# Expert products in tiles of 32 rows on PE's four column groups, in plain fp32, instead of tiles of 128 rows as three rounded products

## The chip, the cores and the metric

The kernel runs on one core of a Trainium2 chip. The metric is the device time of one execution in microseconds. The core has five engines, each with its own instruction stream: TensorE (PE, matrix products; PEld is its loading of the stationary operand), VectorE (DVE), ScalarE (ACT), GpSimdE (POOL) and SyncE (SP, which here only issues DMAs). They meet through semaphores. PE writes to PSUM, eight banks of 512 fp32 columns in each of 128 partitions.

## The reference

One inference step of a hybrid backbone: 128 context tokens and 512 latent tokens, 1024 channels, one layer. The token mixer (mLSTM, Fourier and pooling branches, merge gates, output projection) is not touched. The change is in the mixture of experts behind it:

```python
p_group = softmax(xf @ w_r1 + b_r1);  g_val, g_idx = top_k(p_group, 1)         # one of 4 groups
fine_sel = (einsum("nd,dge->nge", xf, w_r2) + b_r2)[g_idx]                      # its 4 experts
e_val, e_idx = top_k(fine_sel, 2);  e_w = softmax(e_val) * g_val
dense_w = one-hot of (g_idx * 4 + e_idx), weighted by e_w                       # (n, 16)
hid = einsum("nd,edf->nef", xt, w_up);  a, b = split(hid, 2)                    # 1024 -> 2 x 512
hid = silu(a) * b * dense_w
y = einsum("nef,efd->nd", hid, w_down)                                          # 512 -> 1024
```

Each of the 640 tokens goes to two of 16 experts, so there are 1280 rows of expert work. An expert has 4 MiB of up weights and 2 MiB of down weights in fp32, 96 MiB for all (100.7 MB). With the inputs of the reference the 16 experts get 91, 96, 151, 60, 67, 63, 51, 65, 45, 168, 132, 35, 66, 61, 55 and 74 rows. In tiles of 128 rows, one at least for each expert, that makes 19 tiles; in tiles of 32 rows it makes 3, 3, 5, 2, 3, 2, 2, 3, 2, 6, 5, 2, 3, 2, 2 and 3, together 48.

## The kernel before, in words

The program is straight code up to the output projection. Then, for each block of 128 tokens, LN1 and the router's logits are made, and the modulated rows u2 are written to a scratch tensor in HBM (`u2_rows`). DVE turns the logits into a slot for every (token, choice) (lines 1375 to 1462): experts get whole tiles in turn, so a slot is 128 times the tile number plus a place. It also writes `plan`, a row of integers with the expert of each tile and the number of tiles. PE makes from one-hot matrices the list of the tokens in each tile (`tile_idx`, line 1842).

The expert stage is a loop over tiles on each of PE, ACT, DVE and POOL (`expert_tile`, `gather`), with the trip count read from `plan`. SP has its own loop over experts.

For one tile: POOL gathers its 128 rows of u2 from HBM into `xg` (line 707). PE transposes them, eight 128x128 blocks, into PSUM (line 1851). ACT copies the transposed rows rounded to the fp32r format into `xgT_hi` (line 966), and DVE takes the remainder, the exact rows minus the rounded ones, into `xgT_lo` (line 1468). PE then multiplies with the weights, which stand in the same two parts. `split_product` adds hi*hi, hi*lo and lo*hi: 24 matmuls of 128x512 for the first half of the up weights, 24 for the second, and 24 for down (line 1859, and 1899 for the last tile). ACT makes the sigmoid of the first half (line 993), DVE multiplies by it and by the second half (lines 1484, 1491), PE transposes the hidden rows (line 1886), ACT rounds them (line 1008), DVE takes their remainder (line 1504). The down product of a tile is done one tile later, after the up product of the next, so that PE has work while the hidden rows are prepared. ACT copies its two banks to SBUF and stores 128 rows of 4 KiB in `y_slots` with one DMA (lines 980 to 984).

The weights of the next expert come by DMA, in pieces of 512 KiB, into three staging sets (SP, lines 596 and 609). When the next tile has another expert, ACT rounds each of 12 pieces into its hi place (lines 948, 953) and DVE makes its lo part (lines 1361, 1367). Both are in a conditional block, for which ACT and DVE read three entries of `plan` into registers for each tile (lines 987 to 991, 1476 to 1480). There are six places of 16 KiB per partition for hi and lo parts. A staging piece is free for the next load when its lo part is made.

At the end two rows of y per token are gathered from `y_slots`, weighted, added, and LN2 is made.

The column groups of PE are used in the kernel before too, in the product of the conditioning vectors with w_mod at line 1570. Its stationary operand has 32 columns, and four matmuls in turn write partitions 0 to 31, 32 to 63, 64 to 95 and 96 to 127 of one bank, 512 columns each, in plain fp32. In the profile a plain fp32 matmul has two records, an fp32r matmul one.

## Time and profile before

| | us |
|---|---|
| median of 3 runs (1094.95 to 1096.83) | 1095.31 |
| profiled execution | 1101.74 |
| its span, first to last instruction | 1099.9 |
| PE busy | 947.7 |
| DVE busy | 618.3 |
| ACT busy | 444.0 |
| mean granted PE clock | 0.926 |

The span is that of one profiled execution, 1.8 us shorter than its own device time. The time of the profiled execution is 6.4 us above the median of the runs. Busy times of matmuls overlap in the records, because the shown end of a matmul includes its way through the array. The distance from one start to the next tells what a matmul costs in a row of them. The chain that ended last goes back from the last instruction, at each step to what released it. A PEclk of 1.00 stands for 2.4 GHz and of 0.50 for 1.2 GHz. GB/s counts all DMA traffic of the core.

### The profile page before, as it was taken

Reading aid. Unit: us, or ns where it says so; the run is one execution under the profiler, and the core shown is the slowest. Engines: PE = TensorE matmul, PEld = TensorE weight load, DVE = VectorE, ACT = ScalarE, POOL = GpSimd, SP = SyncE. Lnnn points to the kernel's source line nnn. Section 1 sums busy time; section 2 is a strip of 40 time slices with the busy share of each in tenths; the row PEclk is TensorE's granted clock in tenths of the full one; section 3 lists DMA queues with packets and bytes.
Section 4 is the critical chain, followed back from the end, with each engine's and each line's share of the span. In section 5 each row is a group of like instructions: output and inputs, shape, how many; then the busy total and the mean of one; then the engine's idle time right before and its main releaser. Section 6 shows DMA issues by size and latency. Waiting matters only on the chain.

```text
span 1099.9 us, 13186 instructions
## 1 busy us (share of the span) xinstructions
PE 947.7 (86%) x4547; PEld 750.7 (68%) x4547; DVE 618.3 (56%) x886; ACT 444.0 (40%) x612; POOL 188.2 (17%) x148
## 2 busy tenths in 40 slices
PE   2799699999999999899989973699999999999800
PEld 0588588757777777676657753588888888888600
DVE  4616902023535447413168568486799964889458
ACT  1513212132433434312050003466788854787422
POOL 2386300000000000000005551111111110100056
PEclk9899897999999999989999985799999999999955
DMA  9967646220203013612062044694999977899552
GB/s 328 387 192 289 229 154 249 102 89 1 77 1 115 3 75 24 223 41 77 1 227 79 39 167 139 229 391 173 383 399 398 400 273 273 295 398 375 191 210 96
DMA packets 83107, 214.23 MB, mean 195 GB/s; under 512 B 7871, under 2 KB 9157, under 8 KB 79997
## 3 DMA queue, kind: packets, MB, share of 16 engines
q1 hardware_dynamic: 65072, 165.03, 41.5%
q10 hardware_dynamic: 11564, 26.90, 6.9%
q0 software_dynamic: 6432, 21.79, 5.4%
q8 instruction: 25, 0.41, 0.2%
q14 instruction: 14, 0.11, 0.0%
HBM read 190.59 MB, written 23.11 MB: 194 GB/s over the span
## 4 chain that ended last, share of the span: by engine, by line
PE 72%; DVE 12%; ACT 5%; DMA 4%; POOL 3%; issue 2%; SPq 1%; ACTq 0%; POOLq 0%; DVEq 0%
PE ps L1859 28%; PE ps L1633 23%; PE ps L1550 7%; PE ps L1619 3%; DMA ring<-in_w_mod 2%; PE ps L1750 2%; PE ps L1851 2%; PE ps L1687 1%; DVE R_x L1184 1%; ACT w_hi L772 1%; POOL R_x L666 1%; POOL R_x L665 1%; DMA out<-small 1%; PE ps L1570 1%; PE ps L1744 1%
## 5 line engine op out<-in xcount | busy, mean ns | idle before, releaser
L1633 PE MATMUL ps<-w_hi,uT_hi 128*128 128x512 f32 x320 | 133.4, 417 | 6.4 <-ACT R_x L869 2.5
L1139 DVE TENSOR_TENSOR w_lo<-ring,w_hi 128x1024 fp32r<-128x1024 f32 x52 | 67.0, 1317 | 126.1 <-ACT w_hi L772 124.8
L1633 PE MATMUL ps<-w_lo,uT_hi 128*128 128x512 f32 x320 | 126.8, 396 | 0.0
L687 POOL TENSOR_TENSOR R_u<-R_m 128x1024 f32<-128x1024 f32 x1 | 2.4, 2407 | 464.9 <-DVE R_m L1328 464.9
L1633 PEld LDWEIGHTS ps<-w_hi,uT_hi 128*128 128x128 f32 x320 | 61.0, 191 | 23.2 <-issue 4.0
L1361 DVE TENSOR_TENSOR wa_lo<-ring,wa_hi 128x1024 fp32r<-128x1024 f32 x64 | 74.1, 1219 | 4.4 <-ACT wa_hi L948 4.0
L1633 PEld LDWEIGHTS ps<-w_lo,uT_hi 128*128 128x128 f32 x320 | 60.9, 190 | 13.5
L1859 PE MATMUL ps<-wa_hi,xgT_hi 128*128 128x512 f32 x152 | 63.0, 415 | 5.2 <-DVE xgT_lo L1468 5.2
L869 ACT ACTIVATE R_x<-ps 128x512 f32<-128x512 f32 x30 | 17.9, 596 | 117.8 <-PE ps L1633 117.8
L772 ACT CAST w_hi<-ring 128x1024 fp32r<-128x1024 f32 x52 | 53.4, 1053 | 29.8 <-PE ps L1633 15.6
L1228 DVE TENSOR_TENSOR R_x<-R_x,ps 128x512 f32<-128x512 f32 x20 | 13.8, 688 | 91.0 <-PE ps L1550 90.7
L1633 PE MATMUL ps<-w_hi,uT_lo_a 128*128 128x512 f32 x160 | 64.5, 403 | 0.0
L1633 PE MATMUL ps<-w_hi,uT_lo_b 128*128 128x512 f32 x160 | 62.3, 390 | 0.0
L948 ACT CAST wa_hi<-ring 128x1024 fp32r<-128x1024 f32 x64 | 62.2, 1049 | 0.0
L703 POOL COPY idx_now<-tile_idx 128x1 int32 (+1 forms) x19 | 12.1, 634 | 287.1 <-PE ps L1851 264.3
L1859 PE MATMUL ps<-wa_hi,xgT_lo 128*128 128x512 f32 x152 | 61.1, 402 | 0.0
L1859 PE MATMUL ps<-wa_lo,xgT_hi 128*128 128x512 f32 x152 | 60.7, 399 | 0.0
L1859 PE MATMUL ps<-wb_hi,xgT_lo 128*128 128x512 f32 x152 | 59.3, 390 | 0.0
L1859 PE MATMUL ps<-wb_hi,xgT_hi 128*128 128x512 f32 x152 | 59.1, 389 | 0.0
L1859 PE MATMUL ps<-wb_lo,xgT_hi 128*128 128x512 f32 x152 | 59.1, 389 | 0.0
L1859 PE MATMUL ps<-wd_hi,hidT_hi 128*128 128x512 f32 x144 | 57.5, 399 | 0.0
L1859 PE MATMUL ps<-wd_hi,hidT_lo 128*128 128x512 f32 x144 | 56.2, 390 | 0.0
(356 smaller groups left out, 2216.7 us busy)
## 6 DMA issues: line engine op xcount, KB each, us to landing
ring<-in_w_up SPq DMA_DIRECT2D x64, 512.0 KB, 8.8
ring<-in_w_in SPq DMA_DIRECT2D x11, 2048.0 KB, 8.1
R_d<-in_w_up SPq DMA_DIRECT2D x32, 512.0 KB, 11.0
R_p<-in_w_down SPq DMA_DIRECT2D x32, 512.0 KB, 9.7
R_h<-in_w_down SPq DMA_DIRECT2D x32, 512.0 KB, 10.3
R_d<-in_w_mod SPq DMA_DIRECT2D x13, 1024.0 KB, 5.3
y_slots<-R_m ACTq DMA_DIRECT2D x19, 512.0 KB, 6.2
ring<-in_w_mod SPq DMA_DIRECT2D x8, 1024.0 KB, 21.0
```

Source lines behind the costliest of these rows:

```text
L772: nc.scalar.copy(split_weights(name)[0][:, 2 * q:2 * q + 2], weights(name)[:, 2 * q:2 * q + 2]).then_inc(S["w_hi_done"], 1)
L869: release(nc.scalar.activation(gate_sb[:, s % 2], bank(0), ACT.Sigmoid), ("G", s))
L948: nc.scalar.copy(w_hi_lo[i][0][:, q * PIECE:(q + 1) * PIECE], stage(i, q)).then_inc(S["up_hi"], 1)
L1139: tt(lo[:, at], weights(name)[:, at], hi[:, at].bitcast(F32), ALU.subtract).then_inc(S["w_split"], 1)
L1228: release(tt(dst if b == 1 else gated, gate_sb[:, s % 2], bank(1), ALU.mult), ("Y", s))
L1361: tt(w_hi_lo[i][1][:, at], stage(i, q), w_hi_lo[i][0][:, at].bitcast(F32), ALU.subtract).then_inc(S["up_split"], 1)
L1550: i = mm(out, lhs(k), rhs(k), start=(k == 0), stop=(k == n - 1))
L1619: i = mm(bank(gbank((part, c_, s)))[:, 0:HALF], (hi, lo)[a][:, k, c_ * P:(c_ + 1) * P], uT_parts(k)[b][:, half_cols(s)], start=(k == 0 and ...
L1633: i = mm(out, parts(k)[a][:, tok(j)], w[b][:, k], start=(k == 0 and a + b == 0), stop=(k == KD - 1 and b == 1))
L1750: i = mm(ps[:, b0 + h // 2, (h % 2) * HE:(h % 2) * HE + HE], lhs(h), rhs(h), start=True, stop=True)
L1851: i = tr(bank(4 + d // 4)[:, (d % 4) * P:(d % 4) * P + P], xg[:, d * P:(d + 1) * P], ident)
L1859: i = mm(out, lhs[a][:, k * P:(k + 1) * P], rhs[b][:, k, n0:n0 + BW], start=(k == 0 and a + b == 0), stop=(k == n - 1 and a == 1))
```

## The change

The expert stage is rewritten; the stages before it and after it compute the same.

- A tile has 32 rows (`SUB`), and two tiles make a pair, over which the loops run. A pair has 64 slots, and `MAXP` is the largest number of pairs. The slots, `plan` and `tile_idx` are made for this size.
- One gather fetches both tiles of a pair: each of its 128 indices names half a row of u2 (512 channels), twice the token plus the half. PE needs four transposes for them, ACT one copy of 128x512 (`copy_rows`).
- Nothing is rounded or split. For each 128 channels of the contraction, PE takes 32 rows as the stationary operand and streams 256 columns of weights through each of its four column groups, in plain fp32: 8 steps of four matmuls for up, 4 steps of four for down. The column groups hold different output channels, so that the hidden values are 128x128 and the output rows 128x256.
- The weights are loaded by SP into `staged`, two places of a whole expert used in turn, and copied from there to a third place, `expert_w`, from which PE reads. Of the 12 pieces of an expert ACT copies 0, 2, 4, 8 and 10, and DVE copies 1, 3, 5, 6, 7, 9 and 11. A piece is copied when PE has used the old one for the last time. The first expert's pieces are all copied by ACT.
- An expert's output is stored by four DMAs of 32x256 for each tile. PE too reads two entries of `plan` for each tile, because it waits for the copies of its expert.
- Sigmoid and the two multiplications have 128 columns each. The loads of the last LN's rows are issued by SP, not ACT. To make room, R_d and R_x change places in SBUF.

In the diff, removed lines of the functions printed above are left out, and so are the lines that only change sizes or buffers.

```diff
 GM = 100
-MAXT = NE + (2 * T - NE) // P
+SUB = 32
+MAXS = NE + (2 * T - NE) // SUB
+MAXP = -(-MAXS // 2)
+LAST = 2 * MAXP
+EXPERT = (KD + KF) * 1024
 PIECE = 1024
...
+        staged = spread("staged", 0, 2 * EXPERT).rearrange("p (b q n) -> p b q n", b=2, q=KD + KF)
+        expert_w = spread("expert_w", 2 * EXPERT, EXPERT).rearrange("p (q n) -> p q n", q=KD + KF)
+        up_w = expert_w[:, 0:KD].rearrange("p k (h n) -> p k h n", h=2)
+        down_w = expert_w[:, KD:]
+        xg = R_p[:, 0:BW]
+        xT = R_p[:, BW:2 * BW].rearrange("p (i t) -> p i t", i=4)
+        hid, sig_h, hidT = (R_p[:, 2 * BW + i * P:2 * BW + (i + 1) * P] for i in range(3))
+        y_sb = [R_p[:, 3 * BW + i * 256:3 * BW + (i + 1) * 256] for i in range(2)]
...
+        copies = {"up_by_act": (0, 2, 4), "up_by_dve": (1, 3, 5, 6, 7), "down_by_act": (KD, KD + 2), "down_by_dve": (KD + 1, KD + 3)}
+        copied_by = {q: (name, len(qs), i + 1) for name, qs in copies.items() for i, q in enumerate(qs)}
+        def copied(eng, q, e):
+            name, n, i = copied_by[q]
+            eng.wait_ge(S[name], n * e + i)
...
+            def load_expert(e):
+                up = w_up[0, e].rearrange("(k p) n -> p k n", p=P)
+                down = w_down[0, e].rearrange("(k p) n -> p k n", p=P)
+                for q in range(KD + KF):
+                    if e:
+                        sp.wait_ge(piece_loaded[q], 16 * e)
+                    if e >= 2:
+                        copied(sp, q, e - 2)
+                    src = up[:, q:q + 1, :] if q < KD else down[:, q - KD:q - KD + 1, :]
+                    sp.dma_start(staged[:, e % 2, q:q + 1], src).then_inc(piece_loaded[q], 16)
...
+            def gather(pair):
+                nc.gpsimd.tensor_copy(idx_now[:], tile_idx[:, bass.ds(pair, 1)] if not isinstance(pair, int)
+                                      else tile_idx[:, pair:pair + 1]).then_inc(S["idx_col"], 1)
+                pool.wait_ge(S["idx_col"], pair + 1)
                 nc.gpsimd.tensor_tensor(pool_scratch, const("one"), const("one"), ALU.add)
+                nc.gpsimd.indirect_dma_start(out=xg, out_offset=None, in_=u2_rows.rearrange("t (h n) -> (t h) n", h=2),
                                              in_offset=bass.IndirectOffsetOnAxis(ap=idx_now[:, 0:1], axis=0)
                                              ).then_inc(S["gathered"], 16)
             gather(0)
             pool.wait_ge(S["plan_ready"], 1)
+            pairs = pool.value_load(plan[0:1, LAST:LAST + 1], min_val=NE // 2, max_val=MAXP)
+            with pool.Fori(1, pairs) as pair:
...
+            def copy_piece(q, e, s=None):
+                act.wait_ge(piece_loaded[q], 16 * e + 16)
+                if s is not None:
+                    if q < KD:
+                        act.wait_ge(S["up_step"], KD * s + q + 1)
+                    else:
+                        act.wait_ge(S["down_step"], KF * s + q - KD + 1)
+                src = staged[:, 0, q] if s is None else staged[:, bass.ds(e % 2, 1), q].rearrange("p b n -> p (b n)")
+                act.wait_ge(S["plan_ready" if s is not None else "u2_stored1"], 1)
...
                     take(act, name)
                     release(nc.scalar.copy(u2T[:, j % 2, 4 * k:4 * k + 4].rearrange("p k t -> p (k t)"), bank(2 + k)), name)
+            act.wait_ge(S["x1_ready"], NT)
+            act.wait_ge(S["u2_stored0"], 16 * 3)
+            act.wait_ge(S["u2_stored1"], 16 * 2)
+            for q in range(KD + KF):
+                copy_piece(q, 0)
             act.wait_ge(S["route_neg"], 1)
             nc.scalar.activation(route_a, route_a, ACT.Exp).then_inc(S["route_exp"], 1)
             act.wait_ge(S["route_sel"], 1)
             nc.scalar.activation(route_b, route_b, ACT.Exp).then_inc(S["fine_exp"], 1)
+            def copy_rows(pair):
+                act.wait_ge(S["xT_full"], pair + 1)
+                nc.scalar.copy(xT.rearrange("p i t -> p (i t)"), bank(4)).then_inc(S["xT_ready"], 1)
+            copy_rows(0)
+            def evict(s, i, pair):
+                act.wait_ge(S["down_step"], KF * s + 2 * KF)
+                act.wait_ge(S[f"y_stored{i}"], 64 * pair + (1 if i else 65))
+                nc.scalar.copy(y_sb[i], bank(2)[:, 0:256]).then_inc(S["y_ready"], 1)
+                act.wait_ge(S["y_ready"], s + 1)
+                for g in range(4):
+                    act.dma_start(y_slots[bass.ds(s * SUB, SUB), g * 256:(g + 1) * 256], y_sb[i][SUB * g:SUB * (g + 1), :]
+                                  ).then_inc(S[f"y_stored{i}"], 16)
+            def sub_tile(pair, i, first=False, last=False):
+                s = 2 * pair + i
+                first, last = first and i == 0, last and i == 1
                 e = 0 if first else act.value_load(plan[0:1, bass.ds(s, 1)], min_val=0, max_val=NE - 1)
                 if not first:
                     e_former = act.value_load(plan[0:1, bass.ds(s - 1, 1)], min_val=0, max_val=NE - 1)
                 if not last:
                     e_next = act.value_load(plan[0:1, bass.ds(s + 1, 1)], min_val=0, max_val=NE - 1)
                     with act.If(e_next > e):
+                        for q in copies["up_by_act"]:
+                            copy_piece(q, e_next, s)
                     act.end_ifs()
+                act.wait_ge(S["up_step"], KD * s + KD)
+                nc.scalar.activation(sig_h, bank(0)[:, 0:P], ACT.Sigmoid).then_inc(S["sig_done"], 1)
+                if i == 1 and not last:
+                    copy_rows(pair + 1)
+                if not first:
+                    with act.If(e > e_former):
+                        for q in copies["down_by_act"]:
+                            copy_piece(q, e, s)
                     act.end_ifs()
+                    evict(s - 1, 1 - i, pair)
                 act.wait_ge(S["hT_full"], s + 1)
+                nc.scalar.copy(hidT, bank(6)[:, 0:P]).then_inc(S["hidT_ready"], 1)
             act.wait_ge(S["plan_ready"], 1)
+            pairs = act.value_load(plan[0:1, LAST:LAST + 1], min_val=NE // 2, max_val=MAXP)
+            last = act.value_load(plan[0:1, LAST + 1:LAST + 2], min_val=NE // 2 - 1, max_val=MAXP - 1)
+            for i in range(2):
+                sub_tile(0, i, first=True)
+            with act.Fori(1, last) as pair:
+                for i in range(2):
+                    sub_tile(pair, i)
+            for i in range(2):
+                sub_tile(last, i, last=True)
+            evict(2 * last + 1, 1, last + 1)
+            for i in range(2):
+                act.wait_ge(S[f"y_stored{i}"], pairs * 64 + 65)
             nc.scalar.copy(scratch1[0:1, 3:4], const("one")[0:1, :]).then_inc(S["experts_done"], 1)
             def scale_first(j):
...
+            def copy_piece(q, e, s):
+                dve.wait_ge(piece_loaded[q], 16 * e + 16)
+                if q < KD:
+                    dve.wait_ge(S["up_step"], KD * s + q + 1)
+                else:
+                    dve.wait_ge(S["down_step"], KF * s + q - KD + 1)
+                src = staged[:, bass.ds(e % 2, 1), q].rearrange("p b n -> p (b n)")
+                dve.wait_ge(S["plan_ready"], 1)
+                nc.vector.tensor_copy(expert_w[:, q], src).then_inc(S[copied_by[q][0]], 1)
+            def sub_tile(pair, i, first=False, last=False):
+                s = 2 * pair + i
+                first, last = first and i == 0, last and i == 1
                 e = 0 if first else dve.value_load(plan[0:1, bass.ds(s, 1)], min_val=0, max_val=NE - 1)
                 if not first:
                     e_former = dve.value_load(plan[0:1, bass.ds(s - 1, 1)], min_val=0, max_val=NE - 1)
                 if not last:
                     e_next = dve.value_load(plan[0:1, bass.ds(s + 1, 1)], min_val=0, max_val=NE - 1)
+                    with dve.If(e_next > e):
+                        for q in copies["up_by_dve"][0:3]:
+                            copy_piece(q, e_next, s)
+                    dve.end_ifs()
                 dve.wait_ge(S["sig_done"], s + 1)
+                nc.vector.tensor_tensor(hid, sig_h, bank(0)[:, 0:P], ALU.mult).then_inc(S["silu_done"], 1)
+                dve.wait_ge(S["silu_done"], s + 1)
+                nc.vector.tensor_tensor(hid, hid, bank(0)[:, P:2 * P], ALU.mult).then_inc(S["hid_ready"], 1)
                 if not last:
                     with dve.If(e_next > e):
+                        for q in copies["up_by_dve"][3:]:
+                            copy_piece(q, e_next, s)
                     dve.end_ifs()
+                if not first:
                     with dve.If(e > e_former):
+                        for q in copies["down_by_dve"]:
+                            copy_piece(q, e, s)
                     dve.end_ifs()
             dve.wait_ge(S["plan_ready"], 1)
...
+            def transpose_rows(pair):
+                pe.wait_ge(S["gathered"], 16 * (pair + 1))
+                for k in range(4):
+                    i = tr(bank(4)[:, k * P:(k + 1) * P], xg[:, k * P:(k + 1) * P], ident)
+                i.then_inc(S["xT_full"], 1)
             transpose_rows(0)
+            tr(bank(6)[:, 0:P], ident, ident).then_inc(S["down_step"], KF)
+            def down_product(s, e):
+                pe.wait_ge(S["hidT_ready"], s + 1)
+                for k in range(KF):
+                    copied(pe, KD + k, e)
+                    for g in range(4):
+                        i = mm(ps[SUB * g:SUB * (g + 1), 2, 0:256], hidT[:, SUB * k:SUB * (k + 1)], down_w[:, k, 256 * g:256 * (g + 1)],
+                               start=(k == 0), stop=(k == KF - 1))
+                    i.then_inc(S["down_step"], 1)
+            def sub_tile(pair, i, first=False, last=False):
+                s = 2 * pair + i
+                first, last = first and i == 0, last
+                e = 0 if first else pe.value_load(plan[0:1, bass.ds(s, 1)], min_val=0, max_val=NE - 1)
                 if not first:
+                    e_former = pe.value_load(plan[0:1, bass.ds(s - 1, 1)], min_val=0, max_val=NE - 1)
+                if i == 0:
+                    pe.wait_ge(S["xT_ready"], pair + 1)
+                for k in range(KD):
+                    copied(pe, k, e)
+                    at = 2 * SUB * (k // 4) + SUB * i
+                    for g in range(4):
+                        m = mm(ps[SUB * g:SUB * (g + 1), 0, 0:256].rearrange("p (h n) -> p h n", h=2), xT[:, k % 4, at:at + SUB],
+                               up_w[:, k, :, P * g:P * (g + 1)], start=(k == 0), stop=(k == KD - 1))
+                    m.then_inc(S["up_step"], 1)
+                if not first:
+                    down_product(s - 1, e_former)
                 pe.wait_ge(S["hid_ready"], s + 1)
+                tr(bank(6)[:, 0:P], hid, ident).then_inc(S["hT_full"], 1)
+                if i == 0 and not last:
+                    transpose_rows(pair + 1)
             pe.wait_ge(S["plan_ready"], 1)
```

On PE, the end of one trip of the loop in the kernel before: the last part of a down product, then the transposes of the hidden rows. `wd_hi` and `wd_lo` are the two parts of the down weights, R_m holds the gathered and hidden rows.

```order
L1859 MATMUL ps<-wd_hi,hidT_hi 128x512
L1859 MATMUL ps<-wd_lo,hidT_hi 128x512
L1859 MATMUL ps<-wd_hi,hidT_lo 128x512
L1886 MATMUL ps<-consts,R_m 128x128 x4
L1891 REGISTER_ALU
L1891 COMPARE_AND_BRANCH
```

The same place in the changed kernel, from the transpose of the hidden rows of one tile to the up product of the next. R_p holds the small tiles. "ISA" and "REGISTER_ALU" are work on registers or waits.

```order
L1861 MATMUL ps<-consts,R_p 128x128
L1846 ISA
L1846 TENSOR_LOAD plan
L1846 ISA x2
L1848 TENSOR_LOAD plan
L1848 ISA x2
L519 ISA
L1855 MATMUL ps<-expert_w,R_p 32x256 x4
L519 ISA
L1855 MATMUL ps<-expert_w,R_p 32x256 x4
L519 REGISTER_ALU
```

Four transposes have become one, two reads of `plan` stand ahead of each up product, and register work stands between the steps of four matmuls.

On ACT, the store of a tile in the kernel before: both halves of the output, one DMA, and the rounding of the hidden rows.

```order
L980 COPY R_m<-ps 128x512
L981 REGISTER_ALU
L982 COPY R_m<-ps 128x512
L984 ISA
L984 DMA y_slots<-R_m 128x1024
L1008 CAST hidT_hi<-ps 128x512
```

The same place in the changed kernel.

```order
L984 COPY R_p<-ps 128x256
L987 ISA
L987 DMA y_slots<-R_p 32x256
L987 ISA
L987 DMA y_slots<-R_p 32x256
L987 ISA
L987 DMA y_slots<-R_p 32x256
L987 ISA
L987 DMA y_slots<-R_p 32x256
L1013 COPY R_p<-ps 128x128
```

Two copies of 512 columns have become one of 256, and one DMA has become four, all ahead of the copy of the hidden rows.

## Rows read from the trace of the kernel before

**Rows 1.** The page's chain that ended last, by line.

```profile
PE ps L1859 28%; PE ps L1633 23%; PE ps L1550 7%; PE ps L1619 3%; DMA ring<-in_w_mod 2%; PE ps L1750 2%; PE ps L1851 2%; PE ps L1687 1%; DVE R_x L1184 1%; ACT w_hi L772 1%; POOL R_x L666 1%; POOL R_x L665 1%; DMA out<-small 1%; PE ps L1570 1%; PE ps L1744 1%
```

**Rows 2.** Chain of waits, expert stage: start us, us, engine, what.

```profile
685.61 5.11 DMA R_m<-u_rows,idx_now
690.85 1.96 PE ps L1851 x8
695.25 8.33 PE ps L1859 x24
713.86 12.83 PE ps L1859 x48
...
745.28 5.46 PE ps L1859 x24
750.74 0.44 PE ps L1886 x4
751.18 10.94 PE ps L1859 x48
762.12 0.87 PE ps L1851 x8
...
1037.44 7.36 PE ps L1899 x24
1044.83 0.59 ACT R_m L982
1045.58 2.65 DMA y_slots<-R_m
```

**Rows 3.** Windows: us, then PE PEld DVE ACT POOL busy, PEclk, DMA share, GB/s.

```profile
714.00:1033.00 319.00, 319.00 (x1500) 265.07 (x1501) 254.38 (x245) 220.22 (x260) 34.80 (x48) 0.99 0.89 333
1033.40:1038.70 5.30, 1.56 (x9) 1.12 (x8) 3.32 (x4) 4.67 (x6) 0.00 (x0) 1.00 0.73 233
1038.70:1042.10 3.40, 3.40 (x10) 2.66 (x9) 2.00 (x2) 0.18 (x1) 0.00 (x0) 0.50 1.00 237
```

**Rows 4.** Timeline of PE, 141 to 145 us: start, us, line, records.

```profile
142.11 1.07 PE L1570 MATMUL ps<-R_d,k_weighted 128*32 128x512 f32 x8
143.00 1.04 PE L1570 MATMUL ps<-R_p,k_weighted 128*32 128x512 f32 x8
143.97 0.56 PE L1619 MATMUL ps<-uT_hi,w_hi 128*128 128x320 f32 x2
```

**Rows 5.** Instructions that read the plan; min/median/max ns, first and last start.

```profile
L991 ACTq TENSOR_LOAD <-plan x18: 273/282/336, 694.2 to 1002.0; - x18
L987 ACTq TENSOR_LOAD <-plan x18: 282/378/890, 711.3 to 1018.9; - x18
L989 ACTq TENSOR_LOAD <-plan x18: 275/394/912, 711.9 to 1019.7; - x18
L1889 PEldq TENSOR_LOAD <-plan x1: 487/487/487, 690.9 to 690.9; - x1
```

**Rows 6.** Line L987 alone: what surrounds its load.

```profile
L987 ACTq FUSED_REGOPS  x19: 37/152/158, 711.6 to 1019.4; - x19
```

**Rows 7.** Groups by line and shape: busy us, mean ns, idle before.

```profile
L819 ACT COPY R_m<-ps 128x128 f32<-128x128 f32 x2 | 0.5, 270 | 0.0
L962 ACT COPY R_p<-ps 128x512 f32<-128x512 f32 x10 | 5.5, 588 | 51.6 <-PE ps L1810 51.6
L1328 DVE TENSOR_SCALAR R_m<-R_m 128x1024 f32<-128x1024 f32 x1 | 0.7, 694 | 0.0
L1262 DVE COPY R_x<-ps 128x129 f32<-128x129 f32 x8 | 1.8, 285 | 12.3 <-PE ps L1750 12.3
```

**Rows 8.** Line L984, the store of a tile: duration min/median/max.

```profile
L984 ACTq FUSED_REGOPS  x19: 51/51/51, 733.7 to 1045.4; - x19
L984 ACTq DMA_DIRECT2D y_slots<-R_m x19: 343/344/427, 733.8 to 1045.6; - x19
```

**Rows 9.** Timeline of ACT, 845.5 to 851 us.

```profile
845.77 3.88 ACT L948 CAST wa_hi<-ring 128x1024 fp32r<-128x1024 f32 x4
```

334 lines of the change are left out of this document (86 added, 248 removed).

## The prediction

> **What bounds the kernel now.** I read the page's chain first, then the chain in order of time over the expert stage, then windows for clock and DMA. The chain by line [rows 1] gives its largest share, 28%, to the expert products of line 1859. In order of time [rows 2] one trip of a tile reads 10.94 us (48 matmuls), 0.87 (transposes of gathered rows), 5.46 (24 matmuls), 0.44 (transposes of hidden rows), together 17.71 us, and no engine but PE stands in it. A matmul of 512 columns costs 10.94 / 48 = 0.228 us. The stage begins at 695.25 with tile 0. That tile has waits in it and lasts until 713.86. Seventeen trips and the last up product follow, then the last down product from 1037.44 to 1044.83: 349.6 us from first matmul to last. From 714 to 1033 PE is never idle, its clock is granted at 0.99 (2.4 GHz), and DMA moves 333 GB/s at a share of 0.89 [rows 3]. So the stage is bound by PE, with DMA not far below it. It changes if PE's work shrinks, and then by whatever comes next.
>
> **PE's part.** Four column groups in plain fp32 stand in this trace at line 1570. Eight records (four matmuls of 512 columns) start at 142.11, the next eight at 143.00 [rows 4]. The four groups run side by side: 0.89 us for all. The new step is the same with 256 columns. I halve 0.89 and add a little for what does not shrink: 0.46 us (bounds 0.445, and 0.89 if nothing shrinks). Twelve steps make 5.5 us. Going back to 128-wide operands costs 143.97 - 143.00 - 0.89 = 0.08 us; I allow 0.2 for both ways. One hidden transpose is 0.44 / 4 = 0.11, half a pair's four gather transposes 0.22. PE needs 6.05 us for a tile of 32 rows, 290 us for 48 of them, against 19 x 17.71 = 336 before. The two reads of `plan` on PE (0.487 us for the one in the trace, [rows 5]) come before the up product. Matmuls already issued should cover them, with the hidden transpose waiting for its input behind a down product of 1.8 us. I cost them at nothing; uncovered, they are 48 x 1.1 = 53 us.
>
> **ACT's part.** ACT now has the same kind of work for each of 48 tiles instead of 19, and it works in order.
> - Three reads of `plan`. Medians are 0.28 to 0.39 us [rows 5], with register work of 0.152 behind each [rows 6]. The first starts of L987 and L989 are 0.6 us apart, the last 0.8. I take 0.62 each, 1.9 us (bounds 1.7 and 2.4).
> - Sigmoid and hidden copy of 128 columns, 0.27 each; output copy of 256, between 0.27 for 128 and 0.59 for 512, 0.37; half of a copy of 128x512 per tile, 0.3 [rows 7]. Together 1.2 us.
> - Four DMA issues. One is 0.344 plus 0.051 of registers [rows 8] and a gap. In the chain 1044.83 + 0.59 = 1045.42 ends the copy, and the transfer starts at 1045.58 [rows 2]. I take 0.52 each, 2.1 us (bounds 1.6 and 2.4).
>
> That is 5.2 us per tile, below PE's 6.05. At each of 15 changes of expert ACT also copies five pieces of 128x1024. Four casts of that size last 3.88 us [rows 9], so 0.95 each, 4.75, and 0.5 for waits. Three copies stand ahead of the sigmoid, two ahead of the output copy. DVE's seven pieces have 0.69 each [rows 7] and stay under ACT's. So an expert with n tiles takes the larger of ACT's 5.2 n + 5.2 and PE's 6.05 n:
> - n = 2 (six experts): 15.6 against 12.1
> - n = 3 (seven): 20.8 against 18.2
> - n = 5 (two): 31.2 against 30.3
> - n = 6 (one): 36.4 against 36.3
>
> The sum is 94 + 146 + 62 + 36 = 338, less 5 because the first expert has no change: 333. The two engines also wait for each other. In the 16 tiles beyond two per expert ACT has nothing to catch up on and goes at PE's pace, 0.85 us more each: 14. This makes 347 us.
>
> **The clock.** While ACT copies ahead of the sigmoid, PE has finished both products and waits some 3 us for hidden rows. The kernel before has such a wait once. From 1033.4 to 1038.7 PE is busy for 1.56 us, and in the next 3.4 us the clock is 0.50, 1.2 GHz [rows 3]. Eight column-group steps then last up to 1.7 us longer. ACT's lag takes some of it back. I take 0.8 us of loss at each of 15 changes, 12 us (bounds 0 and 50). The Trainium skill ("TensorE: Matmul & The Clock Gate", section "HAM oscillation — how this bites in real kernels") describes this pattern: a thin kernel whose bursts of matmuls are parted by waits restarts slowly after each, all through. By it every one of the 15 waits would cost the full 1.7 us, 25 instead of 12.
>
> **Ends of the stage.** Routing loses two wa_lo pieces from DVE's chain and gains longer comparisons on one partition; I estimate 0.7 us less. The first gather is half as large, but the weight queue beside it fuller, so 5.1 us stay [rows 2]. Four transposes instead of eight save 1.0, and the copy of 128x512 takes 0.6, with no remainder behind it. The first up product starts at about 691.9, 3.4 us earlier. Behind the last tile stand one down product (2 us), and three more issues ahead of the final store (1.6 us). The stage ends at 691.9 + 347 + 12 + 2 = 1053 against 1044.8, and the final store 1.6 us later still: 10 us more, 1112 for the profiled execution of 1101.7. The median of the runs is 1095.3. With the same difference I forecast **1106 us**, slower by 1%. Break-even is a mean of 7.3 us per tile of 32 rows; I have 7.5.
>
> **Weights.** 100.7 MB in some 340 us are 296 GB/s, below the 333 of before [rows 3], and the loads run up to two experts ahead. I cost them at nothing.
>
> **Rivals.**
>
> *Faster, ACT hides under PE.* If reads and issues come at their low bounds (1.7 and 1.6), ACT has 4.5 n + 5.2: 14.2 for n = 2, 18.7 for n = 3, and PE's 30.3 and 36.3 for the rest. That is 85 + 131 + 61 + 36 - 5 = 308; with 10 us of mutual waits and no clock loss 318, a stage end near 1014, 30 us less. Halfway from break-even I put it at 1078. It decides at 7.3 us per tile. For it: register work runs while ACT's own copies run, and I counted them one after the other. Against it: L987's loads reach 0.89 us [rows 5].
>
> *PE's own issue is the bound.* A step has 16 records in 0.46 us, 0.029 us each. The densest long row in the trace is the transposes, 8 matmul records with 8 loads in 0.87 us [rows 2], 0.054 each. At 0.054 a step takes 0.87 and the stage 48 x 11 = 528, a time near 1275. With a little only, say 0.55 us a step, PE needs 7.1 us a tile and ACT's copies come on top: 1140. For it: register work stands between the steps. Against it: at line 1570 records start in a bunch, though only 16 in a row. The Trainium skill (same page, section "Wait — 56ns, not 53.3ns?") says that the sequencer spends about 62 ns per MATMUL where decoding isn't done in hardware. Eight of them would be an estimate of 0.50 us a step, and the sum would be 1130. No run here shows which way decoding is done.
>
> *DMA is the bound.* If loads with stores of 1 KiB rows and gathers beside them moved only 270 GB/s, the weights would take 373 us from about 650, and three tiles follow: an end near 1045, no change. Against it: 333 GB/s were moved with pieces of 2 KiB rows, and now they have 4 KiB.
>
> *The groups don't run side by side*, which would make four times 290 us: excluded by [rows 4].
>
> **How the numbers follow.** Forecast 0.48: 1098 to 1122 by itself. Faster rival 0.37, issue-bound PE 0.09 with 1125 to 1275, DMA-bound 0.06 with about 1095. What the measurement can't tell from no change is within 0.2% (2.2 us); the edge of the first two cases and the DMA case give it 0.07. Faster gets 0.38, slower 0.55. The range 1068 to 1142 leaves out the far ends of both sides.
>
> **What would show it.** Right: PE's groups at the new up line with starts 0.46 us apart from step to step at clock 1.00; a trip of two tiles without a change of 12.1 to 13 us, one with a change 16 or more; idle time of PE before the hidden transpose, released by DVE behind ACT's sigmoid; windows of clock 0.50 in the stage; DMA under 320 GB/s. Wrong: no idle time of PE there and changes that cost nothing (faster rival); steps further apart than 0.5 us at full clock with nothing waited for (issue); waits for pieces on `staged` (DMA).

## The result and the profile after

The changed kernel takes 1153.76 us (median of 4 runs, 1146.12 to 1157.02) against 1096.07 for the kernel before in the same job (4 runs, 1094.95 to 1100.07): a ratio of 1.0504, interval 1.0459 to 1.0550. The direction was forecast, the size was not: 58 us slower instead of 11, and outside the range of 1068 to 1142. The profiled execution took 1155.21 us (span 1153.4), 53.5 more than the one of before.

Line numbers below are those of the kernel in question: in the changed kernel L1855 is the up product, L1839 the down product, L1861 the transpose of hidden rows, L1828 that of gathered rows, L1846 and L1848 PE's plan reads, L954 ACT's weight copy, L987 the stores.

The page's chain by engine ("issue" is time in which an engine waited for nothing that the profile shows; it had 2% of the span before):

```profile
PE 59%; DVE 12%; issue 9%; ACT 7%; DMA 6%; ACTq 5%; POOL 3%; SPq 1%; POOLq 0%; DVEq 0%
```

The page's groups (line, engine, operation, operands, count; busy us, mean ns; idle time of the engine ahead of them, and what ended it):

```profile
L1855 PE MATMUL ps<-expert_w,R_p 128*32 128x256 f32 x3072 | 207.3, 430 | 46.8 <-issue 46.3
L954 ACT COPY expert_w<-staged 128x1024 f32 (+1 forms) x87 | 85.6, 1046 | 41.4 <-PE ps L1855 32.3
...
L1861 PE MATMUL ps<-consts,R_p 128*128 128x128 f32 x48 | 15.8, 328 | 37.3 <-DVE R_p L1474 37.2
```

PE's idle time in the stage stands behind the second bar: 46.8 us ahead of the up products, ended by "issue" (nothing that the profile shows was waited for), and 37.3 ahead of the hidden transposes, ended by DVE. A window over the stage (length, then busy of PE, PEld, DVE, ACT, POOL; clock; DMA share; GB/s), to hold against [rows 3]:

```profile
700.00:1100.00 400.00, 311.58 (x4724) 173.63 (x4712) 96.60 (x201) 123.23 (x242) 32.46 (x66) 0.91 0.67 244
```

From 714 to 1033 us PE was never idle before; now it is for 88 of 400 us. The chain in order of time through a change of expert and the plain tile behind it (start us, us, what; the counterpart of [rows 2]):

```profile
845.16 5.22 PE ps L1855 x64
850.37 1.35 PE ps L1839 x24
...
855.56 0.27 ACT R_p L1013
855.89 0.15 ACTq L993
...
859.61 1.04 ACT expert_w L954
860.64 0.18 ACT R_p L1003
860.85 0.30 DVE R_p L1472
861.17 0.30 DVE R_p L1474
861.47 0.04 issue
861.51 0.33 PE ps L1861
861.84 1.74 issue
863.58 6.23 PE ps L1855 x64
869.81 1.73 PE ps L1839 x32
871.54 0.26 PE ps L1861
871.80 0.44 PE ps L1828 x4
872.24 0.26 issue
872.50 3.66 PE ps L1855 x64
876.16 1.73 PE ps L1839 x32
877.88 0.26 PE ps L1861
878.14 1.63 issue
```

Three things are to be seen. ACT's chain runs from its hidden copy at 855.56 over plan reads and three weight copies to the sigmoid at 860.64, while PE waits. The up product behind the wait lasts 6.23 us at a mean granted clock of 0.58; the next one, at full clock, 3.66. And between the last transpose and the next up product stand 1.74 and 1.63 us in which PE waits for nobody. What PE's instruction queue does there is in the view of lines L1846 and L1848, around 862 us (min/median/max ns, first and last start):

```profile
L1846 PEldq TENSOR_LOAD <-plan x1: 310/310/310, 862.0 to 862.0; - x1
L1846 PEldq FUSED_REGOPS  x1: 151/151/151, 862.4 to 862.4; - x1
L1848 PEldq TENSOR_LOAD <-plan x1: 300/300/300, 862.7 to 862.7; - x1
```

The two plan reads, 0.76 us from start to start, stand in PE's queue behind the transpose that waits for hidden rows. That wait ends at 861.51, the first read begins at 862.0, and the up product at 863.58. Behind a wait the reads leave a gap of about 1.8 us, or 0.85 where the transposes of gathered rows follow the hidden one and cover a part. Where PE did not wait the gap is mostly smaller, for instance 1.15 (at 773.26) or 0.23 (at 753.61). A gap stands ahead of all 47 up products that have reads.

The slow up products are the clock's: two windows, each exactly one up product (columns as above), one behind the wait and the next.

```profile
863.58:869.81 6.23, 6.23 (x68) 3.13 (x72) 0.00 (x0) 0.27 (x1) 0.00 (x0) 0.58 1.02 395
872.50:876.16 3.66, 3.66 (x68) 2.31 (x72) 0.08 (x1) 0.51 (x2) 1.33 (x3) 1.00 0.96 329
```

PE is busy for all of both, and 6.23 x 0.58 = 3.6. The same holds for each of the 17 up products that last longer than 3.66 us: no idle time inside, and duration times mean granted clock gives 3.60 to 3.64. They are those of all 15 changes of expert (27.6 us more than full speed in all), the first tile (2.3) and the last tile (1.7).

The stage adds up: 48 up products at 3.66 (175.7), down products at 1.73 (83), transposes 12.5 and 10.9, together 282; gaps ahead of the up products 46.8; waits for hidden rows 37.3; up products slower than 3.66, 207.3 - 175.7 = 31.6; one wait ahead of the last down product 2.6. That is, to rounding, 400 of the 401.2 us between the first up product (696.81) and the end of the last down product (1098.02). Before it was 349.6.

### The profile page after: what moved, and what is told of

The parts are those of the page before. It is cut to its first block, busy times and chain, and to the rows that moved or that the text cites. A ratio compares the mean times of both kernels' runs of the same rounds, so it can differ in the third digit from the quotient of the medians.

```text
span 1153.4 us, 21554 instructions
## 1 busy us (share of the span) xinstructions
PE 922.0 (80%) x7704; PEld 643.9 (56%) x7705; DVE 437.2 (38%) x819; ACT 335.1 (29%) x580; POOL 179.6 (16%) x163
## 4 chain that ended last, share of the span: by engine, by line
PE 59%; DVE 12%; issue 9%; ACT 7%; DMA 6%; ACTq 5%; POOL 3%; SPq 1%; POOLq 0%; DVEq 0%
PE ps L1610 21%; PE ps L1855 13%; PE ps L1527 6%; PE ps L1839 4%; PE ps L1596 3%; ACTq L987 2%; ACT expert_w L954 2%; DMA ring<-in_w_mod 2%; PE ps L1727 2%; PE ps L1664 1%; DMA R_p<-u_rows,idx_now 1%; DVE R_x L1182 1%; ACT w_hi L773 1%; POOL R_x L667 1%; POOL R_x L666 1%
## 5 line engine op out<-in xcount | busy, mean ns | idle before, releaser
L1855 PE MATMUL ps<-expert_w,R_p 128*32 128x256 f32 x3072 | 207.3, 430 | 46.8 <-issue 46.3
L1855 PEld LDWEIGHTS ps<-expert_w,R_p 128*32 128x32 f32 x3072 | 108.8, 123 | 132.8 <-issue 88.8
L1472 DVE TENSOR_TENSOR R_p<-R_p,ps 128x128 f32<-128x128 f32 x48 | 13.8, 288 | 252.0 <-ACT R_p L1003 252.0
L954 ACT COPY expert_w<-staged 128x1024 f32 (+1 forms) x87 | 85.6, 1046 | 41.4 <-PE ps L1855 32.3
L1839 PE MATMUL ps<-expert_w,R_p 128*32 128x256 f32 x1536 | 91.8, 379 | 2.6 <-ACT R_p L1013 2.6
L1457 DVE COPY expert_w<-staged 128x1024 f32 x105 | 69.0, 693 | 53.2 <-PE ps L1855 41.5
L1839 PEld LDWEIGHTS ps<-expert_w,R_p 128*32 128x32 f32 x1536 | 50.7, 110 | 34.7 <-ACT R_p L1013 2.8
L773 ACT CAST w_hi<-ring 128x1024 fp32r<-128x1024 f32 x52 | 53.4, 1053 | 30.1 <-PE ps L1610 15.9
L704 POOL COPY idx_now<-tile_idx 128x1 int32 (+1 forms) x24 | 6.9, 287 | 343.1 <-PE ps L1828 320.7
L1596 PE MATMUL ps<-uT_hi,w_hi 128*128 128x320 f32 x192 | 46.6, 325 | 8.1 <-DVE w_lo L1137 8.1
L1003 ACT ACTIVATE R_p<-ps 128x128 f32<-128x128 f32 x48 | 13.1, 274 | 118.5 <-PE ps L1855 114.8
L1861 PE MATMUL ps<-consts,R_p 128*128 128x128 f32 x48 | 15.8, 328 | 37.3 <-DVE R_p L1474 37.2
```

The lines of the kernel that those rows point to most:

```text
L773: nc.scalar.copy(split_weights(name)[0][:, 2 * q:2 * q + 2], weights(name)[:, 2 * q:2 * q + 2]).then_inc(S["w_hi_done"], 1)
L954: nc.scalar.copy(expert_w[:, q], src).then_inc(S[copied_by[q][0]], 1)
L1457: nc.vector.tensor_copy(expert_w[:, q], src).then_inc(S[copied_by[q][0]], 1)
L1596: i = mm(bank(gbank((part, c_, s)))[:, 0:HALF], (hi, lo)[a][:, k, c_ * P:(c_ + 1) * P], uT_parts(k)[b][:, half_cols(s)], start=(k == 0 and ...
L1839: i = mm(ps[SUB * g:SUB * (g + 1), 2, 0:256], hidT[:, SUB * k:SUB * (k + 1)], down_w[:, k, 256 * g:256 * (g + 1)], start=(k == 0), stop=(k ...
L1855: m = mm(ps[SUB * g:SUB * (g + 1), 0, 0:256].rearrange("p (h n) -> p h n", h=2), xT[:, k % 4, at:at + SUB], up_w[:, k, :, P * g:P * (g + 1 ...
```

## Experiments

Theory A: the step costed at nothing, PE's plan reads, is on the path. Rival B: ACT's serial work sets the pace, and PE's gap only fills a wait. Rival C: the clock behind each wait. Up to the first gather the kernels of this table are the same program but for an instruction or two, yet the first gather was issued anywhere from 680.2 to 688.6 us in their profiled executions. So beside the times stands the stage's own length, first up product to end of the last down product, and its parts from the view of groups:

| kernel | us (median) | ratio to before, interval | stage | idle ahead of up | up busy | idle ahead of hidden transposes |
|---|---|---|---|---|---|---|
| changed | 1153.8 | 1.050 (1.046 to 1.055) | 401.2 | 46.8 | 207.3 | 37.3 |
| e1 PE reads early | 1113.9 | 1.015 (1.010 to 1.019) | 363.2 | 0.5 | 196.0 | 56.4 |
| e2 one store | 1134.5 | 1.033 (1.031 to 1.036) | 385.3 | 43.1 | 202.1 | 30.9 |
| e3 ACT one read | 1123.8 | 1.025 (1.021 to 1.028) | 376.8 | 42.3 | 196.7 | 24.2 |
| e4 all three | 1063.4 | 0.969 (0.963 to 0.974) | 317.2 | 0.5 | 181.3 | 28.6 |
| e5 PE one read, in place | 1122.1 | 1.020 (1.016 to 1.023) | 371.7 | 8.8 | 196.7 | 52.2 |
| e6 = e1, PE kept busy | 1094.2 | 0.995 (0.993 to 0.997) | 343.5 | 0.5 | 176.9 | 16.3 |
| e7 small copies | 1080.1 | 0.983 (0.981 to 0.985) | 328.7 | 41.4 | 177.8 | 1.1 |
| e8 = e4, piece behind sigmoid | 1063.7 | 0.967 (0.964 to 0.970) | 312.4 | 3.6 | 179.8 | 20.1 |
| e9 = e8, weights held | 1059.9 | 0.965 (0.963 to 0.968) | 312.1 | 3.6 | 179.0 | 20.2 |
| e10 = e8, store by POOL | 1156.7 | 1.054 (1.051 to 1.057) | 401.3 | 1.6 | 204.5 | 2.9 |
| e11 = e9 + e10 | 1156.7 | 1.053 (1.050 to 1.055) | 407.6 | 1.6 | 206.2 | 2.9 |
| e12 = e11, POOL's order mended | 1036.3 | 0.944 (0.942 to 0.947) | 286.5 | 1.5 | 178.1 | 2.6 |

**e1, PE's reads early.**

```diff
-                e = pe.value_load(plan[0:1, bass.ds(s, 1)], ...)
-                e_former = pe.value_load(plan[0:1, bass.ds(s - 1, 1)], ...)
+                e_former, e = (pe.snap(r, ...) for r in (then, now))
+                turn(2 * pair - 1)             
+                up_product(pair, 0, e)
+                down_product(2 * pair - 1, e_former)
+                e_odd = read_plan(2 * pair + 1)
+                turn(2 * pair)
...
+                pe.reg_mov(then, e_odd)
+                pe.reg_mov(now, read_plan(2 * pair + 2))
```

Here `turn` waits for hidden rows and transposes them.

> The changed kernel with one edit on PE: the plan entry of the next tile is read before PE waits for the hidden rows, and the entries already read are kept in registers, so no read stands between a hidden transpose and the next up product. Theory A (PE's two reads stand uncovered, because PE takes its instructions in order and reaches them only behind the transpose that waits for hidden rows): the idle time of PE ahead of the up products, 47.0 us in 48 tiles of the changed kernel, falls under 10 us; a part of it comes back as longer waits ahead of the hidden transposes (35 us in 18 tiles now, up to 20 more), so the kernel is 22 to 38 us faster than the changed one: 1116 to 1132. Rival B (ACT's serial work sets the pace, PE's reads only fill a wait): the waits ahead of the hidden transposes grow by nearly all of it, to about 80 us, and the time falls by less than 8 us: above 1146. Rival C (the clock after each wait): up products behind a change stay at 5.3 us, no change of the time beyond 10 us.

39.9 us faster than the changed kernel, 38.0 of them in the stage, slightly more than A's bound.

```profile
L1853 PE MATMUL ps<-expert_w,R_p 128*32 128x256 f32 x3072 | 196.0, 412 | 0.5 <-ACT R_p L977 0.5
L1859 PE MATMUL ps<-consts,R_p 128*128 128x128 f32 x48 | 16.2, 337 | 56.4 <-DVE R_p L1474 56.3
```

The idle time ahead of the up products went from 46.8 to 0.5. Of these 46 us, 19 came back as waits for hidden rows (37.3 to 56.4), and 11 more were won because up products got faster (207.3 to 196.0; why, e6 tells). Rival B is out as the whole answer: only the 19 us that came back are its part. So is rival C, whose bound was 10 us, though at 11 of the 15 changes the up product still lasts 4.5 to 6.1 us. The edit does two things at once: it takes the reads early, and it makes one read of two for each tile. What each is worth, e5 tells.

**e2, one store for a tile.**

```diff
-                for g in range(4):
-                    act.dma_start(y_slots[bass.ds(s * SUB, SUB), g * 256:(g + 1) * 256], y_sb[i][SUB * g:SUB * (g + 1), :]
-                                  ).then_inc(S[f"y_stored{i}"], 16)
+                act.dma_start(y_slots[bass.ds(s * SUB, SUB), :].rearrange("t (g n) -> g t n", g=4), y_sb[i]
+                              ).then_inc(S[f"y_stored{i}"], 16)
```

> The changed kernel with one edit on ACT: the output of a tile leaves by one DMA of 128 KB, where there were four of 32 KB, so ACT issues 48 and not 192. Theory A: ACT's issues (0.5 us each, 1.6 us less per tile) matter only where PE waits for hidden rows at a change, 8 to 20 us faster than the changed kernel: 1134 to 1146. Rival B (ACT's serial work sets the pace): three issues fewer are 48 x 1.6 = 77 us of ACT's time, over 30 us faster: below 1124.

19.3 us faster, inside A's bounds. But one issue is not as cheap as I took it. The view of the store's line in the changed kernel and in this one (min/median/max ns):

```profile
L987 ACTq DMA_DIRECT2D y_slots<-R_p x191: 321/327/1302, 711.7 to 1099.7; - x191
```

```profile
L986 ACTq DMA_DIRECT2D y_slots<-R_p x48: 555/1050/1125, 704.3 to 1075.5; - x48
```

Four of 32 rows cost 4 x 0.33 and some 0.2 of register work each; one of 128 rows costs 1.05. ACT saves 1.0 us a tile, not 1.6. The rows alone don't make the issue long: the kernel before issued 128 rows of 4 KiB in 0.344 us [rows 8].

**e3, ACT reads once.** The plan entries stay in registers; the one read left stands ahead of ACT's wait for transposed hidden rows.

```diff
-                e = act.value_load(plan[0:1, bass.ds(s, 1)], ...)
-                e_former = act.value_load(plan[0:1, bass.ds(s - 1, 1)], ...)
-                e_next = act.value_load(plan[0:1, bass.ds(s + 1, 1)], ...)
...
+                e_after = read_plan(s + 2)
                 act.wait_ge(S["hT_full"], s + 1)
```

> The changed kernel with one edit on ACT: one plan read for a tile where there were three, taken before ACT waits for the transposed hidden rows, the others kept in registers. Theory A: the chain from hidden copy over reads and three weight copies to the sigmoid gets 1.7 us shorter at 15 to 18 tiles, and only there: 10 to 28 us faster than the changed kernel, 1126 to 1144. Rival B: over 30 us faster, below 1124. If ACT's reads are covered by the wait for the up product: no change.

30.0 us faster (24.4 in the stage), 2 us beyond A's bound and just at B's ("over 30", below 1124, measured 1123.75): the time alone doesn't decide between them. The stage does. Two reads fewer, at 0.62 us each, are 60 us of ACT's time in 48 tiles, and the stage gave back 24.4; the other 5.6 us lie outside it, in code that is the same. The gap of PE stays (42.3); waits for hidden rows and slow up products shrink, 37.3 to 24.2 and 207.3 to 196.7.

**e4, the three together.**

> All three edits together: PE's reads early, one store, one read on ACT. Theory A: with both kinds of idle time gone PE's own 6.05 us a tile is what is left, 290 us and some rest at changes; the stage ends 75 to 95 us earlier, and the kernel is at 1060 to 1080, faster than the kernel before. Rival C (the clock): the up products behind a change stay at 5.3 us instead of 3.66 although the waits are short, 30 us of loss stay, 1080 to 1100. Rival D (DMA): below 300 us for the stage the weights (100.7 MB) arrive too late, PE's copies wait for the staged pieces, and the time stops near 1065.

90.3 us faster than the changed kernel and 3.1% faster than the kernel before. In the stage the three alone gave 38.0, 15.9 and 24.4, in sum 78.3; together they give 84.0. So PE's reads and ACT's chain are two costs side by side, and not one hidden behind the other. D's number, near 1065, fits this time as well; e8 shows what there is to it, and e12 that the time doesn't stop there. C's 30 us of slow up products did not stay: 181.3 - 175.7 = 5.6 is left.

**e5, one read on PE in the old place.** As e1, but each read stands behind the transposes (the odd tile's is shown, the even tile's moves likewise).

```diff
-                e_odd = read_plan(2 * pair + 1)
                 turn(2 * pair)
                 if not final:
                     transpose_rows(pair + 1)
+                e_odd = read_plan(2 * pair + 1)
```

> The changed kernel with one plan read on PE where there were two, at the old place behind the transposes, the entry of the tile before kept in a register. The early reads made the changed kernel 40 us faster. Theory A (each read left on the path costs its own 0.75 us for every tile): the idle time ahead of the up products falls from 47 us to 10 to 20, and the kernel is 22 to 32 us faster than the changed one, 1122 to 1132, between it and the kernel with early reads (1114). Rival (only the place counts, one uncovered read stalls PE as long as two): 1150 or more.

31.7 us faster than the changed kernel, 8.2 slower than e1 with the same number of reads.

```profile
L1853 PE MATMUL ps<-expert_w,R_p 128*32 128x256 f32 x3072 | 196.7, 413 | 8.8 <-issue 7.9 <-ACT R_p L977 0.5
```

The idle time is 8.8 us, a little under the 10 to 20 expected. One read leaves 0.6 us uncovered where PE has just waited for hidden rows and transposes no gathered rows (two reads leave 1.8 there), and about 0.2 or less in nearly all other tiles. So most of e1's gain, 31.7 of 39.9 us, is had by reading once instead of twice, and the early place gives the other 8.2. Two reads in the early place were not run.

**e6, PE kept busy at a change (on e1).**

```diff
+            def keep_busy(change):
+                with pe.If(change):
+                    for _ in range(24):
+                        tr(bank(7)[:, 0:P], ident, ident)
+                pe.end_ifs()
```

> The kernel with early reads on PE (1113.9 us), and at each change of expert 24 transposes of a constant into an unused PSUM bank between the down product and the wait for hidden rows, 2.6 us of PE work that nobody uses. Theory C (the slow up products behind a change, 196.0 us in 48 where 175.7 is full speed, are slow because the clock is granted at 0.50 after the wait): they stay at 3.66 us, 18 to 20 us less; the added work costs 1 us at the few changes whose wait is shorter, and the kernel comes to 1096 to 1104. Rival (they are slow because the weight copies of the new expert come late): 196 stays, and the time is 1114 to 1122.

19.7 us faster than e1, in the time and in the stage, 2 us beyond C's bound:

```profile
L1853 PE MATMUL ps<-expert_w,R_p 128*32 128x256 f32 x3072 | 176.9, 383 | 0.5 <-ACT R_p L977 0.5
```

Up products went from 196.0 to 176.9 us with the same weight copies. (The waits for hidden rows, 16.3 in the table, are only what the added transposes leave of them.) At all 15 changes the up product now lasts 3.66 us. So in e1 the slow up products are the clock's work, and 24 transposes at each change that nobody reads are worth 20 us.

**e7, small copies.** This kernel leaves out most of each weight copy and prices the rest.

```diff
-                nc.vector.tensor_copy(expert_w[:, q], src).then_inc(S[copied_by[q][0]], 1)
+                nc.vector.tensor_copy(expert_w[:, q, 0:8], src[:, 0:8]).then_inc(S[copied_by[q][0]], 1)
 (the same on ACT)
```

> The changed kernel, in which the weight copies at a change of expert move 8 columns of each piece instead of 1024, so that all waits and counts stay and only the time of the copies goes; the experts after the first compute with wrong weights. It prices the copies to the third place. Theory: ACT's three copies ahead of the sigmoid (3.1 us) are most of the waits ahead of the hidden transposes (35.3 us) and by them of the slow clock behind (31.6 us): 45 to 65 us faster than the changed kernel, 1089 to 1109; the idle time ahead of the up products stays at 45 or more. If ACT's reads and issues make the waits: less than 25 us faster.

73.6 us faster, more than expected.

```profile
L1855 PE MATMUL ps<-expert_w,R_p 128*32 128x256 f32 x3072 | 177.8, 384 | 41.4 <-issue 41.0
L1861 PE MATMUL ps<-consts,R_p 128*128 128x128 f32 x48 | 15.8, 329 | 1.1 <-DVE R_p L1474 1.1
```

Without the copies' time both the waits (37.3 to 1.1) and the slow clock (207.3 to 177.8) are gone, and PE's gap is still there. That is the copies' whole price, 72.5 us of the stage. The expectation had left out that a shorter chain on ACT takes nearly every wait away, not "most".

**e8, the third up piece behind the sigmoid (on e4).** ACT copies pieces 0 and 2 ahead of the sigmoid, piece 4 behind it.

> The kernel with all three edits (1063.4 us), and on ACT the third of the three up pieces copied behind the sigmoid instead of ahead of it. The waits left there ahead of the hidden transposes are 26.4 us, 1.5 to 2.4 at each change. Theory: the sigmoid then starts about 1 us earlier at each of 15 changes, waits fall to 8 to 14 us, 12 to 18 us faster: 1045 to 1051. Rival (DMA, 371 GB/s from 800 to 850 us in the trace of the three edits): pieces arrive late, waits for staged pieces take the place, less than 5 us faster.

Missed: 1063.7 us, the same as e4. The waits did get 0.9 to 1.0 us shorter at 12 of the 15 changes, and the stage is 4.8 us shorter, but 28.6 fell only to 20.1 (8 to 14 expected), and e8's profiled first gather came 5.3 us later than e4's, in code that is the same. Two things took the rest back. The piece behind the sigmoid also stands ahead of ACT's copy of the gathered rows (L977), so at six changes PE waited 0.53 us for that copy, 3.2 in all. And one wait is new, seen in the waits from 846 to 862 us (who, what, released by: us, times, longest):

```profile
DVE expert_w L1470 <- DMA staged<-in_w_up: 6.1, 4, 2.6
PEld ps L1872 <- DVE R_p L1487: 6.1, 1, 6.1
PE ps L1872 <- DVE R_p L1487: 5.6, 1, 5.6
```

DVE copies weight pieces ahead of the hidden product, here they were late from DRAM, and the product stood behind them in DVE's order. So part of the DMA rival was right. A third wait was there in e4 already and is the largest that DMA causes in e8 (waits from 700 to 1005 us):

```profile
ACT R_p L984 <- DMA y_slots<-R_p: 20.0, 10, 3.0
PE ps L1866 <- ACT R_p L977: 3.2, 6, 0.5
```

ACT's output copy waits until the store from the same buffer, two tiles before, has landed: 20.0 us in ten waits, 14.8 in eight in e4, none in the changed kernel and none in e12. It stands in ACT's order ahead of the hidden copy. So there are two reasons why moving the stores off ACT can help, the time of the issue and this wait, and no run tells them apart.

**e9, weights held for the first gather (on e8).**

```diff
+                if e == 2:
+                    sp.wait_ge(S["gathered"], 16)
```

> The kernel before this one (three edits and the third up piece behind the sigmoid, 1063.7 us), with one edit on SP: the weights of the third expert are not asked for until the first gather has landed. In all kernels of this case the first gather takes 6.35 us beside 400 to 410 GB/s of weights, and the first up product starts 8.2 us behind its issue; the kernel before the change had 5.1 us. Theory: the gather shrinks to 3 to 5 us and the first up product comes 1.5 to 3 us earlier behind the issue; but 15 us of DMA time are given up, the weights have less lead, and waits for staged pieces appear behind tile 20: within 5 us of 1063.7. Rival (latency and not the beside traffic makes the gather long): 6 us stay.

1059.9 against 1063.7 us; the intervals overlap, but the chain of waits shows the edit. First the changed kernel, then e9:

```profile
688.57 6.35 DMA R_p<-u_rows,idx_now
694.91 0.14 issue
695.05 1.10 PE ps L1828 x4
```

```profile
681.01 3.43 DMA R_p<-u_rows,idx_now
```

Without weights beside it the gather takes 3.43 us instead of 6.35 (6.34 in e8): the DMA share over it is 0.26 here and was 1.03, at 408 GB/s, in the changed kernel. The kernel before had held some of its weight loads for the first gather too; the DMA share over its 5.11 us was 0.34, for twice the bytes. The first up product stands 5.3 us behind the issue (686.34) instead of 8.2. The stage itself is as long as e8's, with the late pieces at tile 24 again.

**e10 and e11, the store by POOL.**

```diff
 (ACT's evict ends with the copy to y_sb; POOL, in each trip)
                 next_rows(pair)
+                store(2 * pair - 3, 1)
+                store(2 * pair - 2, 0)
```

> The kernel with three edits and the third up piece behind the sigmoid (1063.7 us), with the output's DMA issued by POOL instead of ACT. On ACT one DMA of 128 rows of 1 KiB lasted 1.04 us (each of the four of 32 rows 0.35 to 0.45), so 1.2 us per tile leave ACT's chain, the one that ends in hidden copy, weight copies and sigmoid. Theory: waits ahead of the hidden transposes fall from 17.9 us to 4 to 10 us, no piece of the stage is above 6.1 us a tile but where DMA is late: 1050 to 1058. Rival (DMA is the bound now): waits for staged pieces grow instead, 1060 or more. POOL's gathers may come later behind its stores: then waits ahead of the transposes of gathered rows show it.

> Both of the last two edits together: weights of the third expert held for the first gather, and stores issued by POOL. Theory: gains of both as far as the weights keep up, 1046 to 1056. If DMA is the bound, holding the loads costs what the stores gain: 1060 to 1066.

Both missed by some 100 us, by my order on POOL. ACT's part did what was expected: waits for hidden rows went from 20.1 to 2.9. But tile 2 * pair - 2 is evicted one tile too late for the next gather, which now stood behind its store. Groups and chain of e10:

```profile
L1857 PE MATMUL ps<-consts,R_p 128*128 128x128 f32 x96 | 21.2, 359 | 86.8 <-DMA R_p<-u_rows,idx_now 86.8
```

```profile
808.21 0.08 POOL y_slots L723
...
809.52 7.05 DMA R_p<-u_rows,idx_now
816.57 0.04 issue
816.62 1.11 PE ps L1857 x4
817.73 4.61 PE ps L1882 x64
```

The store goes out at 808.21, only then the gather at 809.52, and PE waits for it until 816.62. In the stage these waits are 79 us (the rest of the 86.8 stands ahead of it). e10 is 93 us slower than e8, as much as the whole of what e4 and e8 had won.

**e12, POOL's order mended (on e11).** Gather first, then the stores of two tiles that were evicted a tile earlier.

```diff
-            with pool.Fori(2, pairs) as pair:
-                next_rows(pair)
-                store(2 * pair - 3, 1)
-                store(2 * pair - 2, 0)
+            with pool.Fori(0, before_last) as done:
+                next_rows(done + 2)
+                store(2 * done, 0)
+                store(2 * done + 1, 1)
```

> Weights held and stores issued by POOL as in the kernel of both, with POOL's order mended: in the kernel of both POOL issued a pair's gather behind a store whose output PE makes one tile later, and PE waited 79 us for gathered rows (22 times, longest 5.8). Now POOL issues in each trip the gather first and then the stores of two tiles that are ready one tile earlier. Theory: the waits for gathered rows go to under 5 us, those ahead of the hidden transposes from 18.0 us to 7 to 12, of which 6.3 are one wait for late weights at tile 24; 1048 to 1056, and the fastest kernel. Rival (POOL's DMAs cost ACT's gain again, by stores that land late or by DVE and POOL disturbing each other): 1060 or more.

1036.3 us, 5.6% faster than the kernel before (ratio 0.9444, 0.9421 to 0.9468) and better than expected: the late weights at tile 24 are gone too. Why they are wasn't separated.

```profile
L1892 PE MATMUL ps<-consts,R_p 128*128 128x128 f32 x48 | 15.7, 328 | 2.6 <-DVE R_p L1507 2.2 <-issue 0.2
```

```profile
800.00:850.00 50.00, 49.26 (x841) 28.37 (x833) 20.92 (x42) 27.19 (x49) 13.10 (x21) 1.00 1.03 402
850.00:900.00 50.00, 50.00 (x868) 28.88 (x856) 9.56 (x25) 14.54 (x34) 12.22 (x21) 1.00 1.02 399
```

From 850 to 900 us PE is busy for 50.00 of 50 us at full clock, and in the whole stage it is idle for 4.6 us. The stage is bound by PE again, at 286.5 / 48 = 5.97 us a tile, with DMA right below it: share 0.95 from 700 to 975 us. The prediction gave PE's part as 6.05.

## Why the prediction failed, step by step

- **PE's work, right.** A step of four column groups takes 3.66 / 8 = 0.46 us in the up product and 1.73 / 4 = 0.43 in the down product, forecast 0.46. PE's part is 5.9 to 6.0 us a tile against 6.05. The rival of PE's issue for each matmul fell with it, since no step is above 0.46 us at full clock. The Trainium skill (TensorE: Matmul & The Clock Gate, "Wait — 56ns, not 53.3ns?") gives about 62 ns per MATMUL for a sequencer without hardware decode. The trace has eight in 0.43 us, 54 ns each, so that price does not bind here.
- **PE's plan reads, the step that failed.** "Matmuls already issued should cover them ... I cost them at nothing; uncovered, they are 48 x 1.1 = 53 us." They stand in the queue behind the transpose that waits for hidden rows, and when that wait ends too little that was issued is left to cover them. They cost 46.8 us of idle time, an idle time that shrinks to 8.8 with one read in the same place (e5) and to 0.5 with one early read (e1), which gave 38.0 us of the stage back. I had the price (48 x 1.1) and the place (ahead of the up product), and didn't ask what stands before them in the queue.
- **ACT's part and the waits, right in kind, close in part by luck.** e1 is the kernel that I had priced. Its stage is 363.2 us, forecast 347 + 12 + 2 = 361. Its waits for hidden rows are 56.4 us, forecast 57 (347 less 290). The time, 1113.9, lies in the forecast's own range of 1098 to 1122. Three errors cancel in part in that. The rows counted six experts with two tiles and seven with three; the lists in the section on the reference have seven and six, and 7 x 15.6 + 6 x 20.8 makes the sum 5 us smaller (342 for 347, a forecast of 1101). PE's own work was put 8 us too high, and slow up products in e1 are 20.3 us (196.0 less 175.7) where 12 were forecast. The terms behind it hold to a tenth: three reads from the hidden copy at 855.56 to about 857.3, weight copies of 1.05 us where I had 0.95, an issue of 0.33 with 0.2 around it where I had 0.52.
- **The clock, too small.** 12 us were forecast for the 15 changes. e6 shows 19 in e1 (196.0 less 176.9). In the changed kernel it is 31.6, of them 27.6 at the 15 changes, 1.8 each, and all of it is clock by the granted clock of each product. That PE's own gap of 0.6 to 1.8 us behind each wait makes it more than in e1 is likely, but not shown. The Trainium skill (same page, "HAM oscillation — how this bites in real kernels") describes waits, longer ones than these, that restart PE slowly each time; by it the forecast would have been 25. The changed kernel agrees, with a slow up product at 15 of 15 changes. But not every wait costs: in e1 it was 11 of 15, and in e4 two of 15.
- **The start, partly right.** The up product begins 8.2 us behind the first gather's issue, 9.6 before (695.25 less 685.61, [rows 2]): 1.4 us won, not 2.7. The gather took 6.35 us, not 5.1, and e9 shows that the weights beside it did that; the 5.1 had been read from a gather with nothing beside it (103 GB/s in its window, which is its own 512 KiB).
- **The weights, right for this kernel.** 244 GB/s in the stage; no wait for `staged` that matters until the stage had shrunk to 312 us.
- **The rivals.** The faster one, ACT hidden under PE, came true only once ACT's reads and issues had been cut and its order changed (e12). My chance of 0.38 for faster rested on ACT's terms alone.

The sum of the miss: the stage is 40 us longer than forecast (401.2 against 361). PE's reads are 46.8 of it and the slow up products 19.6 (31.6 less 12); waits for hidden rows give 19.7 back (37.3, not 57), because PE is late anyway, and PE's own work 8 (282 against 290); 2.6 is the wait ahead of the last down product. These add to 41.3, a little more than the 40. Another 4.9 is the later start (696.81 against 691.9), of which the later first gather of this execution (688.57, 685.61 before) is 3.0 and the longer gather 1.25.

## What to carry to other kernels

PE's reads of a value were covered here only by work that was already issued when they ran, so look for what the instruction queue holds in front of it: behind a wait, little is left. Read once what can be kept in a register (31.7 us here), and read it ahead of the wait (8.2 more). Where one engine's instruction order carries copies, reads, issues and the one operation another engine waits for, put that one first. With fewer reads and issues, the weights held for one gather, and another order and place for the rest, the same copies and products went from 1154 to 1036 us. And a store moved to an idle queue is moved in front of whatever that queue does next: one tile too early on POOL cost 93 us against e8, and mending the order gave 120 (e11 to e12).
